# Statistics ahead of norm weights, two more banks for transposes, and the first feed-forward products around the last tiles' transposes, in an encoder layer on one core

## The chip, the cores and the metric

The kernel runs on one core of a Trainium2 chip. The metric is the device time of one execution in microseconds. TensorE is written PE, VectorE DVE, ScalarE ACT, GpSimd POOL, and SP is the engine that issues the DMAs.

## What is computed

One layer over 2048 tokens of width 1024, all in float32:

```python
def reference(x, mem, ...):
    x = layer_norm(x, ln0_g, ln0_b)
    for l in range(DEPTH):          # DEPTH = 1
        y = mixer(x, mem, w_in[l], ..., w_out[l])      # x @ w_in (1024 -> 1408), conv, pooling, attention, @ w_out
        x = layer_norm(DEEPNORM_ALPHA * x + y, ln1_g[l], ln1_b[l])
        y = conv_ffn(x, w_up[l], ...)                  # w_up 1024 -> 5632, conv of width 3, gated, w_down -> 1024
        x = layer_norm(DEEPNORM_ALPHA * x + y, ln2_g[l], ln2_b[l])
    return x
```

## The kernel before

Every float32 matrix product is made of three products of rounded parts: each operand is split into a high part (ACT copies it to fp32r, the names end in `hi`) and a low part (DVE subtracts the high part from the raw value, the names end in `lo`). So each stationary or moving operand needs one ACT copy and then one DVE subtraction before PE can use it. The order of the work on each engine is written out by hand; the engines wait for each other by semaphores, and each engine and SP's queue take their work strictly in this order.

**The opening and the input projection** (`project_phase`). The 2048 tokens are four chunks of 512, each of four tiles of 128 tokens (`TT`). For a tile, DVE's `layer_norm` takes the statistics (two `bn_stats`, one `bn_aggr`) and then subtracts the mean and multiplies with the norm weight (L389); POOL makes the reciprocal deviation; `layer_norm_end` (L395) multiplies with it and adds the norm bias. PE's `turn` transposes half a tile into one of the two PSUM banks `tp` (L264), ACT's `split_hi` copies the half out (L319), DVE's `split_lo` makes the low part (L401) and thereby frees the bank: `turn(c, i)` waits for the low part of half tile i-2. The weights `w_in` come in ten pieces (`load_w`), split by `weights_hi` (L324) and `weights_lo` (L406). In chunk 0 the first four of the eleven column tiles are projected in two halves of 256 tokens (`project_half`, L293), each half going through four weight pieces; the rest by `project` (L279). `turns_behind` says behind which column tile of a chunk the transposes of the next chunk stand: in chunk 0, behind the last four.

**The handover to the feed-forward part.** In the middle phase chunks are 256 tokens (`NCH` = 8, so the last is number 7, with two tiles). For its tile u, `residual` adds (L1616), `statistics` follows, POOL makes the deviation (`rstds`), ACT applies it (`norm`, L1341), DVE multiplies and adds the norm weights (`affine`, L1626 and L1627), PE transposes (`turn_x1`, L1073, into two banks), ACT copies out (`turned_x1`, L1459), four sums of the transposed quarters follow (`operand_sums`), and SP stores seven operands per chunk (`store_operands`).

The feed-forward products use a scheme of seven block products for what would be eight. A block (`Blk`) has seven stationary operands (`up.hi`, L2262, and `up.lo`, L2401; four of them from sums of raw quadrants, `held_sums`) and shares seven moving operands (`load_moving`, through three staging slots `mov_raw`; `up.moving_hi`, L2269, and `up.moving_lo`, L2405). Product j needs stationary and moving operand j. Product 0 goes to one bank, which ACT also copies to a second (`preset`); product 2 adds to this second one. `keep_u2` and `keep_u4` copy out intermediate results behind products 2 and 4, and product 6 waits for DVE's `up_c22` (L2428); ahead of that, `clear_edge` (L2604) writes to memory that the stores of the last operands must have left. PE's own order at the handover is at L1262 to L1277: the last projections, `turn_x1` of tile 0 of the last chunk, two matmuls that open banks, product 0, product 1, `turn_x1` of tile 1, then `rest` (products 2, 3, 4, product 0 of the second block, 5, 6). The four sums of the last chunk are made by POOL (`last_operand_sums`), those of all others by DVE.

## Time and profile before

| | us |
|---|---|
| median of 3 runs | 1945.98 |
| lowest and highest run | 1945.35, 1946.87 |
| profiled execution, its own time | 1944.67 |
| its span (first to last instruction) | 1943.0 |
| PE busy in the span | 1871.2 (96%) |
| DVE, ACT, POOL busy | 1474.6, 940.0, 221.2 |

The span is what the rows count from; the profiled execution's time is 1.67 us more, and the median of the runs is 1.31 us above that execution. PE is the busiest engine in nearly every part of the span, so time is to be looked for where PE stands idle or runs at the lower of its clock's levels. A row of the timeline has the start in us, the duration in us, the engine, the line of the kernel, the operation, what it writes and reads, and, in brackets, the idle time of the engine before it and what ended that. Where many like instructions are merged into one row, the duration is that of the group.

### The profile page before, as it was taken

The numbers are of one execution on the slowest core, as the hardware profiler recorded it, in microseconds if no ns is written. First come the engines' busy times: TensorE is split into PE (matmuls) and PEld (weight loads), VectorE is DVE, ScalarE is ACT, GpSimd is POOL, SyncE is SP. The second block draws the span as 40 slices with busy tenths as digits, with TensorE's granted clock in tenths as the row PEclk, the third lists the DMA queues.
The fourth block names the chain that finished last, engine by engine and source line by source line (L and its number), as shares of the span: only waits on it lengthen the run. The fifth ranks groups of instructions, "written<-read, shape, count | busy, mean of one in ns | idle before, by whom it ended". The sixth has DMA issues, their size and how long they took to land.

```text
span 1943.0 us, 26237 instructions
## 1 busy us (share of the span) xinstructions
PE 1871.2 (96%) x8722; PEld 1558.2 (80%) x8722; DVE 1474.6 (76%) x1927; ACT 940.0 (48%) x1598; POOL 221.2 (11%) x311
## 2 busy tenths in 40 slices
PE   6999999899999899999999899999999998999998
PEld 5788889688888688888888788888887786887886
DVE  6544228878887988888888987777878768567999
ACT  2311115746564565656556656555566335225231
POOL 1111014200000212121220020000000000000112
PEclk9999999999999999999999999999999999999999
DMA  6432226555345634434345432121215668457443
GB/s 227 168 109 71 60 79 212 185 160 187 133 153 186 253 124 143 141 135 140 130 143 175 148 140 108 76 86 76 97 69 179 226 211 292 165 173 278 177 155 127
DMA packets 171931, 296.13 MB, mean 152 GB/s; under 512 B 11728, under 2 KB 106192, under 8 KB 171856
## 3 DMA queue, kind: packets, MB, share of 16 engines
q1 hardware_dynamic: 171856, 295.18, 43.6%
q8 instruction: 42, 0.69, 0.1%
q14 instruction: 33, 0.27, 0.0%
HBM read 189.23 MB, written 105.91 MB: 152 GB/s over the span
## 4 chain that ended last, share of the span: by engine, by line
PE 62%; DVE 13%; DMA 4%; issue 3%; ACT 2%; SPq 0%; POOL 0%; DVEq 0%; ACTq 0%; POOLq 0%
PE banks L2200 49%; PE banks L1109 7%; DVE mov_lo L2405 2%; DVE sta_lo L2401 2%; DMA y_scratch<-up_and_out 2%; PE banks L1137 1%; DMA mov_raw<-in_w_down 1%; DVE up_and_out L2452 1%; PE banks L1042 1%; PE banks L1091 1%; ACT mov_hi L2269 1%; DVE up_and_out L2439 1%; PE banks L1118 1%; DVE up_and_out L2436 1%; PE banks L1062 1%
## 5 line engine op out<-in xcount | busy, mean ns | idle before, releaser
L2200 PE MATMUL banks<-mov_hi,sta_hi 128*128 128x512 f32 x1848 | 724.1, 392 | 25.0 <-DVE mov_lo L2405 9.1
L2200 PE MATMUL banks<-mov_hi,sta_lo 128*128 128x512 f32 x1848 | 721.7, 391 | 0.0
L2200 PE MATMUL banks<-mov_lo,sta_hi 128*128 128x512 f32 x1848 | 721.1, 390 | 0.0
L2200 PEld LDWEIGHTS banks<-mov_hi,sta_hi 128*128 128x128 f32 x1848 | 348.4, 189 | 106.9 <-issue 16.7
L2200 PEld LDWEIGHTS banks<-mov_hi,sta_lo 128*128 128x128 f32 x1848 | 348.1, 188 | 73.0
L2200 PEld LDWEIGHTS banks<-mov_lo,sta_hi 128*128 128x128 f32 x1848 | 348.5, 189 | 71.8
L2262 ACT ACTIVATE sta_hi<-sta_raw 128x512 fp32r<-128x512 f32 (+1 forms) x340 | 198.5, 611 | 144.3 <-PE banks L2200 98.2
L2401 DVE TENSOR_TENSOR sta_lo<-sta_raw,sta_hi 128x512 fp32r<-128x512 f32 (+1 forms) x340 | 224.0, 675 | 40.6 <-ACT sta_hi L2262 38.6
L279 PE MATMUL banks<-x0t_hi,win_hi 128*128 128x512 f32 x320 | 126.5, 395 | 1.6 <-DVE x0t_lo L401 1.6
L2291 ACT ACTIVATE half_sums<-banks 128x512 f32<-128x512 f32 x68 | 40.7, 598 | 179.4 <-PE banks L2200 179.4
L279 PE MATMUL banks<-x0t_hi,win_lo 128*128 128x512 f32 x320 | 124.8, 390 | 0.0
L279 PE MATMUL banks<-x0t_lo,win_hi 128*128 128x512 f32 x320 | 124.6, 389 | 0.0
L2439 DVE SCALAR_TENSOR_TENSOR up_and_out<-up_and_out,ffn_conv_w 128x1024 f32<-128x1024 f32 x88 | 113.1, 1285 | 11.2 <-DVE up_and_out L2436 5.5
L2432 DVE TENSOR_TENSOR up_and_out<-banks,half_sums 128x512 f32<-128x512 f32 x44 | 30.4, 691 | 115.9 <-PE banks L2200 115.9
L2334 ACT ACTIVATE up_and_out<-up_and_out,ffn_conv_b,ffn_conv_w 128x1024 f32<-128x1024 f32 x88 | 109.6, 1245 | 17.1 <-ACT up_carry L2317 7.8
L2436 DVE SCALAR_TENSOR_TENSOR up_and_out<-up_and_out,ffn_conv_w 128x1024 f32<-128x1024 f32 x88 | 112.5, 1278 | 0.0
L2282 ACT ACTIVATE half_sums<-banks 128x512 f32<-128x512 f32 x68 | 40.7, 598 | 143.6 <-PE banks L2200 130.1
L1109 PE MATMUL banks<-wout_hi,mix_hi 128*128 128x512 f32 x240 | 96.1, 400 | 1.0 <-DVE mix_lo L1604 1.0
L1109 PE MATMUL banks<-wout_hi,mix_lo 128*128 128x512 f32 x240 | 93.7, 390 | 0.0
L1109 PE MATMUL banks<-wout_lo,mix_hi 128*128 128x512 f32 x240 | 93.4, 389 | 0.0
L2401 DVE TENSOR_TENSOR sta_lo<-sta_sums,sta_hi 128x512 fp32r<-128x512 f32 (+1 forms) x136 | 92.9, 683 | 0.0
L2405 DVE TENSOR_TENSOR mov_lo<-mov_raw,mov_hi 128x2048 fp32r<-128x2048 f32 (+1 forms) x35 | 77.1, 2209 | 17.8 <-ACT mov_hi L2269 17.8
(242 smaller groups left out, 2706.0 us busy)
## 6 DMA issues: line engine op xcount, KB each, us to landing
sta_raw<-in_w_up SPq DMA_DIRECT2D x88, 512.0 KB, 4.2
hidden_scratch<-up_and_out SPq DMA_DIRECT2D x44, 512.0 KB, 2.6
y_scratch<-up_and_out SPq DMA_DIRECT2D x16, 1024.0 KB, 7.3
sta_raw<-hidden_scratch SPq DMA_DIRECT2D x32, 512.0 KB, 4.4
up_and_out<-y_scratch SPq DMA_DIRECT2D x16, 1024.0 KB, 4.9
x_operands<-x_operands_out SPq DMA_DIRECT2D x56, 256.0 KB, 4.3
mov_raw<-x_operands SPq DMA_DIRECT2D x14, 1024.0 KB, 7.8
mov_raw<-in_w_down SPq DMA_DIRECT2D x44, 256.0 KB, 4.6
```

Of the source, the lines that this page charges most:

```text
L279: last = pe.matmul(wb[:, done % 6, :], w, x, start=(k == 0 and i == 0), stop=(k == KT - 1 and i == 2))
L1109: last = pe.matmul(ps_y[:, b, :], w, x, start=(k == 0 and i == 0), stop=(k == KT - 1 and i == 2))
L2200: last = pe.matmul(psum, w, x, start=(start and k == 0 and i == 0), stop=(stop and k == m - 1 and i == 2), skip_group_check=True)
L2262: act.activation(sa_hi[j][:, 0:PAIRS[b.st], :], held(b, j), ACT.Copy).then_inc(sta_hi[j], 1)
L2282: act.activation(u[:, 0, :], ps[:, 2 + b.r, :], ACT.Copy).then_inc(u2, 1)
L2291: act.activation(u[:, 1, :], ps[:, 2 + b.r, :], ACT.Copy).then_inc(u4, 1)
L2334: act.activation(cv[:, w, :], ub[:, w, 0:HT], ACT.Identity, scale=fw[:, w, bass.ds(b.i, 1), 0], bias=fb[:, w, bass.ds(b.i, 1)]).then_inc(t ...
L2401: dve.tensor_tensor(sa_lo[j][:, 0:m, :], held(b, j), sa_hi[j][:, 0:m, :].bitcast(F32), ALU.subtract).then_inc(sta_lo[j], 1)
L2405: dve.tensor_tensor(moving(mv_lo, st, j), staged(st, j), moving(mv_hi, st, j).bitcast(F32), ALU.subtract).then_inc(mov_lo_ok, 1)
L2432: dve.tensor_tensor(tokens(b, VALUE, 0), bank(4 + b.r), u[:, 0, :].rearrange("p (q t) -> p q t", t=P), ALU.add).then_inc(c21, 1)
L2436: dve.scalar_tensor_tensor(out=cv[:, w, :], in0=ub[:, w, P:P + HT], scalar=fw[:, w, bass.ds(b.i, 1), 1], in1=cv[:, w, :], op0=ALU.mult, op ...
L2439: dve.scalar_tensor_tensor(out=cv[:, w, :], in0=ub[:, w, EDGE:EDGE + HT], scalar=fw[:, w, bass.ds(b.i, 1), 2], in1=cv[:, w, :], op0=ALU.mu ...
```

## The change

Seven things are changed.

1. The norm weight and the norm bias get a semaphore each; DVE takes the statistics of tiles 0 and 1 first, then multiplies by the weight (which waits for the weight alone), and waits for the bias only in `layer_norm_end`.
2. In chunk 0, half tiles 2, 3, 6 and 7 are transposed into two more banks (of the six `wb` of the projection), so that `turn(0, i)` waits only from i = 4 on, and for half tile i-4.
3. ACT's copies and DVE's subtractions of the opening are put into another order: transposed half tiles go ahead of weight pieces, and the seventh weight piece goes behind the last half tiles. Half tiles 4 to 7 are transposed behind piece 1 and in the middle of piece 3 of the first half.
4. The transposes of chunk 1 stand behind column tiles 6 to 9 and not 7 to 10, and the low parts of its half tiles are made between the norms and not after all of them.
5. At the handover PE opens the banks and makes product 0 ahead of `turn_x1` of tile 0, makes product 1 after waiting for one residual less, and products 2 and 3 ahead of `turn_x1` of tile 1.
6. ACT and DVE follow: `preset` ahead of the copies of tile 0, stationary and moving operand 3 ahead of `norm` and `affine` of tile 1, and `turned_x1` of tile 1 behind `keep_u2`.
7. The last operand sums go from POOL to DVE, and the load of moving operand 6 goes ahead of the stores of the last tile.

```diff
                 dst = mix_d[row:row + P, :].rearrange("p (r h q) -> p r h q", r=PHASES, h=2)[:, 4 * (c % 2):4 * (c % 2) + 4, c // 2, :]
                 sp.dma_start(dst, qb[:, t, :].rearrange("p (u q) -> p u q", u=TT)).then_inc(q_stored, 16)
 
+        def turned(c, i):
+
+            return wb[:, 4 + i % 2, :] if c == 0 and i % 4 >= 2 else tp[:, i % 2, :]
+
         def turns_behind(c, n):
 
             if c + 1 == NCH:
                 return ()
             if c == 0:
-                return (2 * (n - JT + TT), 2 * (n - JT + TT) + 1) if n >= JT - TT else ()
+                u = n - (JT - TT - 1)
+                return (2 * u, 2 * u + 1) if 0 <= u < TT else ()
             return (n - 1,) if 1 <= n <= 2 * TT else ()
 
         @block.sync
...
             load_x(0)
             load_x(1)
-            for n, v in enumerate((a["ln0_g"], a["ln0_b"])):
-                sp.dma_start(g_b[:, n, :], v.rearrange("(o n) -> o n", o=1).to_broadcast((P, D))).then_inc(gb_loaded, 16)
+            sp.dma_start(g_b[:, 0, :], a["ln0_g"].rearrange("(o n) -> o n", o=1).to_broadcast((P, D))).then_inc(g_loaded, 16)
+            sp.dma_start(g_b[:, 1, :], a["ln0_b"].rearrange("(o n) -> o n", o=1).to_broadcast((P, D))).then_inc(b_loaded, 16)
             for i in range(4):
                 load_w(i)
             load_x(2)
...
                 u, b = i // 2, i % 2
                 n = c * TT + u
                 pe.wait_ge(x0_ready, n + 1)
-                if 2 * TT * c + i >= 2:
+                if c == 0:
+                    if i >= 4:
+                        pe.wait_ge(lo_done, i - 3)
+                else:
                     pe.wait_ge(lo_done, 2 * TT * c + i - 1)
                 for k in range(4):
-                    last = pe.transpose(tp[:, b, k * P:(k + 1) * P], x0[:, n % RING, (4 * b + k) * P:(4 * b + k + 1) * P], ident[:, :])
+                    last = pe.transpose(turned(c, i)[:, k * P:(k + 1) * P], x0[:, n % RING, (4 * b + k) * P:(4 * b + k + 1) * P], ident[:, :])
                 last.then_inc(tp_ready, 1)
...
                                 last = pe.matmul(wb[:, n, tok], w, x, start=(k == 0 and i == 0), stop=(k == KT - 1 and i == 2), skip_group_check=True)
                         if half and piece == 3:
                             last.then_inc(proj, 1)
-                    if half == 0 and piece in (1, 2):
-                        turn(0, 2 * piece + 2)
-                        turn(0, 2 * piece + 3)
+                        if half == 0 and (piece, n) in ((1, 3), (3, 1)):
+                            turn(0, 3 + piece)
...
                 ins.then_inc(evac, 1)
 
             weights_hi(0)
-            weights_hi(1)
             split_hi(0, 0)
             split_hi(0, 1)
-            weights_hi(2)
             split_hi(0, 2)
             split_hi(0, 3)
-            for i in range(3, 7):
+            weights_hi(1)
+            for i in range(2, 6):
                 weights_hi(i)
             for i in range(TT, 2 * TT):
                 split_hi(0, i)
+            weights_hi(6)
             for c in range(NCH):
                 for n in range(JT):
...
                 dve.bn_stats(s[:, 6:12], x[:, 512:1024]).then_inc(ln_part, 1)
                 dve.wait_ge(ln_part, n + 1)
                 dve.bn_aggr(s[:, 12:14], s[:, 0:12]).then_inc(ln_var, 1)
+
+            def layer_scale(n):
+                s, x = st[:, n % RING, :], x0[:, n % RING, :]
                 dve.wait_ge(ln_var, n + 1)
-                dve.wait_ge(gb_loaded, 32)
+                dve.wait_ge(g_loaded, 16)
                 dve.scalar_tensor_tensor(out=x, in0=x, scalar=s[:, 12:13], in1=g_b[:, 0, :], op0=ALU.subtract, op1=ALU.mult).then_inc(ln_scaled, 1)
+
+            def layer_norm(n):
+                layer_stats(n)
+                layer_scale(n)
 
             def layer_norm_end(n):
                 s, x = st[:, n % RING, :], x0[:, n % RING, :]
+                dve.wait_ge(b_loaded, 16)
                 dve.wait_ge(ln_scaled, n + 1)
                 dve.wait_ge(ln_rstd, n + 1)
                 dve.scalar_tensor_tensor(out=x, in0=x, scalar=s[:, 14:15], in1=g_b[:, 1, :], op0=ALU.mult, op1=ALU.add).then_inc(x0_ready, 1)
...
                     layer_norm(c * TT + u)
                     layer_norm_end(c * TT + u)
 
-            layer_norm(0)
-            layer_norm(1)
+            layer_stats(0)
+            layer_stats(1)
+            layer_scale(0)
             layer_norm_end(0)
+            layer_scale(1)
             layer_norm_end(1)
+            lows(0, 0, 1)
             weights_lo(0)
-            lows(0, 0, 1)
+            lows(0, 2, 3)
             weights_lo(1)
-            lows(0, 2, 3)
             layer_norm(2)
-            layer_norm(3)
             layer_norm_end(2)
             weights_lo(2)
+            layer_norm(3)
             weights_lo(3)
             layer_norm_end(3)
             lows(0, 4, 5)
-            weights_lo(4)
             lows(0, 6, 7)
-            for i in range(5, 7):
+            for i in range(4, 7):
                 weights_lo(i)
             for c in range(NCH):
                 if c == 0:
                         weights_lo(i)
                     norms(1, 0)
                     norms(1, 1)
+                    lows(1, 0, 1)
                     gate(0, 1)
                     norms(1, 2)
+                    lows(1, 2, 3)
                     gate(0, 2)
                     norms(1, 3)
-                    lows(1, *range(2 * TT))
+                    lows(1, 4, 5, 6, 7)
                     continue
                 if c + 1 == NCH:
...
             sp.wait_ge(y_used, 2 * TT * NCH)
             up.load_raw(Blk(0, 1, 1))
             up.load_moving(0, 5)
+            up.load_moving(0, 6)
             store_x1(sp, NCH - 1, 1)
             sp.wait_ge(x1t_out, 4 * NCH)
             store_last_operands(sp, ((0, xt[:, 0, 0:4, :]), (3, xt[:, 0, 4:8, :]), (5, xt[:, 1, 4:8, :])), last_xt)
-            up.load_moving(0, 6)
             sp.wait_ge(x1_sums, 4 * NCH)
             store_last_operands(sp, ((1, xs[:, 0, :, :]), (4, xs[:, 1, :, :]), (2, xs[:, 2, :, :]), (6, xs[:, 3, :, :])), xop_stored)
             for s in x1_stored:
...
             pool.memset(half[:, 1:2], EPS).then_inc(half_ok, 1)
             pool.wait_ge(half_ok, 2)
-            def last_operand_sums():
-
-                pool.wait_ge(x1t_out, 4 * NCH)
-                operand_sums(pool, NCH - 1)
-
             def rstds(c):
...
                 project(NCH - 1, 1, n)
                 if n == 0:
                     turn_x1(NCH - 2, 1)
-            for b in range(2):
-                pe.wait_ge(x1t_out, (NCH - 2) * 4 + b + 3)
-            turn_x1(NCH - 1, 0)
             up = ffn.tensor(pe)
             first, second = Blk(0, 0, 0), Blk(0, 1, 1)
             up.open_banks()
             up.product_0(first)
-            pe.wait_ge(y_used, 2 * TT * NCH)
+            for b in range(2):
+                pe.wait_ge(x1t_out, (NCH - 2) * 4 + b + 3)
+            turn_x1(NCH - 1, 0)
+            pe.wait_ge(y_used, 2 * TT * NCH - 1)
             up.product_1(first)
+            up.products_2_3(first)
             turn_x1(NCH - 1, 1)
             up.rest(first, second)
...
             up.hi(first, 2)
             act.wait_ge(y_ready, 2 * TT * NCH)
             up.moving_hi(0, 2)
+            up.preset(first)
             turned_x1(NCH - 1, 0)
-            norm(NCH - 1, 1)
-            up.preset(first)
             up.hi(first, 3)
             up.moving_hi(0, 3)
-            turned_x1(NCH - 1, 1)
+            norm(NCH - 1, 1)
             up.hi(first, 4)
             up.moving_hi(0, 4)
             up.keep_u2(first)
+            turned_x1(NCH - 1, 1)
             up.hi(second, 0)
             up.hi(first, 5)
...
             residual(NCH - 1, 3)
             statistics(NCH - 1, 1)
             up.moving_lo(0, 2)
+            up.lo(first, 3)
+            up.moving_lo(0, 3)
             affine(NCH - 1, 1)
-            for j in (3, 4):
-                up.lo(first, j)
-                up.moving_lo(0, j)
+            up.lo(first, 4)
+            up.moving_lo(0, 4)
             up.lo(second, 0)
             up.lo(first, 5)
             up.moving_lo(0, 5)
             up.lo(first, 6)
+            dve.wait_ge(x1t_out, 4 * NCH)
+            operand_sums(dve, NCH - 1)
             dve.wait_ge(x1t_psum, 4 * NCH)
             for s in x1_stored:
                 dve.wait_ge(s, 16 * NCH)
...
             product(b, 1, ps[:, 4 + b.r, :], True, True)
 
+        def products_2_3(b):
+            pe.wait_ge(y_pre, 1)
+            product(b, 2, ps[:, 2 + b.r, :], False, True)
+            product(b, 3, ps[:, b.r, :], False, True)
+
         def rest(b, after):
-            x, y, z = ps[:, b.r, :], ps[:, 2 + b.r, :], ps[:, 4 + b.r, :]
-            pe.wait_ge(y_pre, 1)
-            product(b, 2, y, False, True)
-            product(b, 3, x, False, True)
```

## Rows read from the trace of the kernel before

**Rows 1.** The chain of work that ended last, share of the span by engine

```profile
PE 62%; DVE 13%; DMA 4%; issue 3%; ACT 2%; SPq 0%; POOL 0%; DVEq 0%; ACTq 0%; POOLq 0%
```

**Rows 2.** Timeline of PE in the opening

```profile
14.68 1.94 PE L264 MATMUL banks<-ident,x 128*128 128x128 f32 x8 [14.68 <-DVE x L395]
...
20.97 0.58 PE L293 MATMUL banks<-x0t_hi,win_hi 128*128 128x256 f32 x1 [1.41 <-DVE x0t_lo L401]
...
35.16 1.22 PE L264 MATMUL banks<-ident,x 128*128 128x128 f32 x8 [2.04 <-DVE x0t_lo L401]
```

**Rows 3.** Timeline of DVE in the opening

```profile
9.28 1.28 DVE L389 SCALAR_TENSOR_TENSOR x<-x,ln_stats,ln_gb 128x1024 f32<-128x1024 f32 x1 [2.88 <-DMA ln_gb<-in_ln_b]
...
13.27 2.47 DVE L395 SCALAR_TENSOR_TENSOR x<-x,ln_stats,ln_gb 128x1024 f32<-128x1024 f32 x2
...
16.79 1.27 DVE L401 TENSOR_TENSOR x0t_lo<-banks,x0t_hi 128x512 fp32r<-128x512 f32 x2
```

**Rows 4.** Timeline of ACT in the opening

```profile
10.55 1.06 ACT L324 ACTIVATE win_hi<-val_gate 128x1024 fp32r<-128x1024 f32 x1 [8.47 <-DMA val_gate<-in_w_in]
...
15.81 0.60 ACT L319 ACTIVATE x0t_hi<-banks 128x512 fp32r<-128x512 f32 x1 [2.84 <-PE banks L264]
...
33.17 0.63 ACT L324 ACTIVATE win_hi<-q_out 128x512 fp32r<-128x512 f32 x1 [8.86 <-DMA q_out<-in_w_in]
```

**Rows 5.** Timeline of SP, then DMA issues with KB and us to landing

```profile
1.72 0.42 SPq L199 DMA_DIRECT2D ln_gb<-in_ln_g  x1
...
ln_gb<-in_ln_g SPq DMA_DIRECT2D x1, 512.0 KB, 6.1
...
x<-in_x SPq DMA_DIRECT2D x2, 512.0 KB, 11.2
```

**Rows 6.** Stretches of L293: length, PE, PEld, granted clock, DMA share, GB/s

```profile
20.97:26.40 5.43, 5.43 (x25) 5.43 (x26) 1.00 0.02 7
...
35.16:40.20 5.04, 4.06 (x21) 4.09 (x22) 0.66 0.76 267
40.20:52.10 11.90, 11.90 (x101) 11.86 (x99) 1.00 0.30 95
```

**Rows 7.** Timeline of PE at the end of chunk 0

```profile
81.56 1.23 PE L264 MATMUL banks<-ident,x 128*128 128x128 f32 x8 [1.18 <-DVE x0t_lo L401]
...
97.11 0.50 PE L279 MATMUL banks<-x0t_hi,win_hi 128*128 128x512 f32 x1 [1.62 <-DVE x0t_lo L401]
```

**Rows 8.** Timeline of PE at the handover

```profile
635.57 1.94 PE L1073 MATMUL banks<-ident,x_out 128*128 128x128 f32 x8 [3.65 <-DVE x_out L1627]
...
653.14 0.47 PE L2200 MATMUL banks<-mov_hi,sta_hi 128*128 128x512 f32 x1 [1.32 <-DVE mov_lo L2405]
```

**Rows 9.** Groups of DVE instructions from 629 to 647: busy us, mean ns

```profile
L2405 DVE TENSOR_TENSOR mov_lo<-mov_raw,mov_hi 128x2048 fp32r<-128x2048 f32 x3 | 6.8, 2268 | 0.0
...
L2401 DVE TENSOR_TENSOR sta_lo<-sta_raw,sta_hi 128x512 fp32r<-128x512 f32 x3 | 2.1, 684 | 0.0
```

**Rows 10.** Groups of DVE instructions from 647.8 to 656.5

```profile
L2401 DVE TENSOR_TENSOR sta_lo<-sta_sums,sta_hi 128x512 fp32r<-128x512 f32 x2 | 3.6, 1785 | 0.0
```

**Rows 11.** Timeline of ACT and of DVE at the handover

```profile
638.10 2.24 DVE L2405 TENSOR_TENSOR mov_lo<-mov_raw,mov_hi 128x2048 fp32r<-128x2048 f32 x1
...
641.42 1.24 ACT L1341 ACTIVATE x_out<-x_out,ln_stats 128x1024 f32<-128x1024 f32 x1 [3.27 <-POOL ln_stats L59]
...
643.60 1.90 ACT L2269 ACTIVATE mov_hi<-mov_raw 128x2048 fp32r<-128x2048 f32 x1
...
661.98 0.63 DVE L2428 TENSOR_TENSOR up_and_out<-banks,half_sums 128x512 f32<-128x512 f32 x1
```

**Rows 12.** SP's issue of moving operand 3; landing of operands 3 and 5

```profile
633.52 0.65 SPq L2040 DMA_DIRECT2D mov_raw<-x_operands  x1
...
mov_raw<-x_operands SPq DMA_DIRECT2D x1, 1024.0 KB, 7.1
...
mov_raw<-x_operands SPq DMA_DIRECT2D x1, 1024.0 KB, 9.7
```

16 lines of the change are left out of this document (9 added, 7 removed).

## The prediction

> **What bounds the kernel now.** I read the shares of the chain of waits first: PE carries 62% of it and DVE 13% [rows 1]. The table gives PE 96% of the span, so a change of order gains only where PE stands idle or at its lower level, and only if nothing later absorbs the shift. Then I read the timelines of the three places that the diff touches.
>
> Opening: PE first works at 14.68, stands idle again ahead of the first projection at 20.97 and for 2.04 us ahead of 35.16 [rows 2]. DVE idles 2.88 us to 9.28 for the norm bias, though its next instruction reads only the weight [rows 3]. The 2.04 us wait starts on ACT: it stood 8.86 us, to 33.17, for the seventh weight piece, which is queued ahead of the transposed half tiles [rows 4]. Behind the wait the granted clock is 0.66 on average over 35.16 to 40.20; in the first stretch 25 matmuls of 256 columns took 5.43 us (0.217 each, the 1.2 GHz level), later 101 took 11.90 (0.118, the 2.4 GHz level) [rows 6]. Chunk 0's end: waits of 1.18 and 1.62 us for DVE's low parts [rows 7]. Handover: PE idle 3.65 us for tile 0 of the last chunk, eight transposes then take 1.94 us (1.22 at the full level in rows 2), and a 1.32 us wait for a moving operand at 653.14 [rows 2, 8]; but product 6 waits for DVE's `up_c22`, done at 662.6 [rows 11]. There DVE, not PE, sets the end.
>
> **Opening, step by step.** Statistics of tile 0 are over at 9.28 - 2.88 = 6.4. Those of tile 1 and its scaling lie between the end of the first scaling, 10.56, and 13.27: 2.7, of which scaling is 1.25, so statistics are 1.5 and now end at 7.9. The weight landed at 1.72 + 6.1 = 7.8 [rows 5]; scaling runs 8.0 to 9.2; the bias has landed by 9.28 [rows 3]; each end step is 1.23 (2.47 for two). Tile 0 is ready at 10.5, not about 14.5, tile 1 at 10.5 + 1.25 + 1.25 = 13.0. POOL's deviation of tile 1 has over 3 us. Transposes of tile 0 start near 10.7, those of tile 1 near 13.15, as no bank is waited for; each pair takes 1.94. ACT's piece 0 (10.55 to 11.6 [rows 4]) is still ahead, but the first half tile's copy starts 1.13 behind its transposes (14.68 to 15.81), at 11.8, so it costs nothing. The last copy ends near 15.7. DVE: end 13.0, two low parts 1.3, weight piece 1.1 (15.74 to 16.79 [rows 3]), low part 3 behind its copy at 16.0, low part 4 to 16.6. The first projection starts at 16.8 instead of 20.97: **-4.2**.
>
> Behind it PE takes 24 matmuls a piece: 5.1 at the lower level to 21.9, piece 1 2.85, half tiles 4 and 5 1.0, piece 2 2.85, half of piece 3 1.4, half tiles 6 and 7 1.0, the rest 1.4: 32.4. DVE, from 16.6: weight piece 1 1.2; tile 2 (landed 5.05 + 11.2 = 16.3 [rows 5]) 2.7 and its end, with POOL between, to 22.3; weight piece 23.5; tile 3 26.2; weight piece 27.35; end 28.6; low parts 4 and 5 29.9. PE needs tile 2 at 24.8, tile 3 at 30.0, piece 3 at 28.6: each is there, with 1.2 us to spare at the narrowest. Low parts 6 and 7 wait for their copies, to 32.6: a new wait of 0.2 to 0.3. So the 2.04 wait goes (**-2.0**), and the lower level behind it too: 16 matmuls x (0.217 - 0.118) = **-1.5**, against **+0.3**. Opening -7.4. Bounds: -5.5, if half a microsecond is lost at each of the four places where a row is extrapolated; -9, if the clock rises 1.6 us sooner than 5.4 us after the start.
>
> **Chunk 0's end.** Transposes of tile 0 of chunk 1 now stand one column tile (5.45 us) earlier; in the old trace tile 4 was ready 2.7 us ahead of that point. DVE carries the four tiles' norms in 4.6 us each, with two low parts (1.3) between, against PE's 5.45 + 0.9 for a column tile and its transposes; it is ahead at each. The last low parts are done some 3 us before PE needs them. Both waits go, and the 0.3 us by which the eight transposes at 81.56 were stretched: **-3.0** (bounds -2.4 and -3.3).
>
> **Handover.** PE no longer idles: banks and product 0 run from 631.8 to 635.0, tile 0's transposes at 635.6, product 1 to 639.2. But its idle time is not what counts; I follow ACT and DVE. DVE is unchanged to 640.3 [rows 11]. ACT now has moving operand 3 ahead of `norm`: its transfer lands at 633.5 + 7.1 = 640.6 [rows 12], the copy takes 1.9 [rows 11], so `norm` starts at 642.6, not 641.42: **a new wait**, behind which stand `affine`, the transposes of tile 1 and the last sums. DVE: low parts of operand 3 to 644.85, `affine` 2.45 (two instructions of 1024 columns, as in rows 3) to 647.3, operand 4 0.6 + 2.2 to 650.1, where product 4 starts, 3 us earlier than 653.14; second block's operand 0 and operand 5's low part to 651.3, moving operand 5 (its load issued when operand 2's low part ends, 640.3 [rows 11], landed 9.7 later [rows 12], copied by 652.3) to 654.5, operand 6's part 655.1 [durations: rows 9, less 0.08 for the overlap of neighbours]. The four sums, now here, are like low parts, 0.65 each: 2.6, to 657.7. Then moving operand 6 to 659.9, clear and add 1.05: 661.0 against 662.6. **-1.6.** That the sums cost DVE 2.6 us and it still ends earlier is because beside POOL's sums its subtractions took 1.79 instead of 0.68 us [rows 9, 10]: four of them, 4.4 us, come back. The stores behind the sums end near 662, and the first reader of their memory stood at 668. Bounds: +1.0 if the transfer lands 2.5 us later; -3.2 if it costs no wait.
>
> The Trainium skill's page "GPSIMD Engine Reference" says in its table of facts that POOL shares its SBUF interfaces with VectorE, with contention where DVE reads two SBUF inputs; rows 10 agree, and by it -1.6 would stand.
>
> **Sum.** -7.4 - 3.0 - 1.6 = -12.0. Projection, middle phase and feed-forward loops wait relative to PE, with no fixed hour, so I keep all of it. The span would be 1931.0, the profiled execution 1932.7; the median of runs lies 1.3 above, so 1945.98 - 12.0 = 1934.0.
>
> **Rivals.** (a) The handover gives nothing or loses up to 1 us: moving operand 3 or 5 lands late and holds `norm` or DVE. For: both landings stand in the sum as waits, and of two loads of 1 MB one took 7.1 and one 9.7 us [rows 12]; 2.5 us more for operand 3 is the bound above. Against: the order of issues is unchanged up to it. Time 1935.6 to 1936.6.
>
> (b) The new short waits at the handover (639.2 to 640.4, 643.2 to 644.9, 648.5 to 650.2) lower the clock. The 2.04 wait did, the 1.32 and 1.62 ones did not [rows 2, 7, 8]; mine go up to 1.7. Price: product 4 at the lower level takes 2.5 us more, of which DVE's queue hides 1.2: +1.3, to 1935.3; with the same thing once in the opening (+1.8) 1937.
>
> (c) The opening gains less: PE starts at 16.8, but the chip stays at the lower level through more of the 192 matmuls. By rows 6 each one costs 0.099 us. Ten more, +1.0. The gain is used up at 121 more; if all 168 behind the first piece and both pairs of transposes (+2.0) run so, it is 16.6 + 2.0 - 12.0 = +6.6: **slower, 1952.6**. Against: it rose after 5.4 us of work in the old trace. The skill's page "TensorE: Matmul & The Clock Gate", Part 1, says that the point of the rise differs from run to run with where the start falls; that would move the time by the bounds of the opening, not to this end.
>
> (d) The opening does not do what it says: ACT or DVE still waits for a weight piece that stands ahead (pieces 2 and 5 land while PE works). If the start stays 1.5 us short and the 2.04 wait stays half, -12.0 + 1.5 + 1.0 + 1.5 = -8.0: 1938.0.
>
> **How the numbers follow.** Forecast, all three parts within their bounds (1931 to 1936): 0.62; (a) 0.15; (b) 0.08; (d) 0.08; more gain than 15 us 0.03; (c) slower 0.02, nearly nothing left 0.02. Range 1930 to 1938.5, about 8 in 10 by these and the doubt in extrapolated rows. A measurement of this kernel tells changes over 0.2% (3.9 us) from none: faster 0.95, same 0.03, slower 0.02.
>
> **What would show it.** First transposes near 10.7, first projection near 16.8, no wait of PE over 0.5 us to the end of the first half, chunk 1 starting near 97.1 - 10.4 = 86.7, and no idle row there. At the handover, all times 10.4 earlier: transposes straight behind product 0, `norm` of tile 1 starting behind the copy of operand 3, three waits of 1 to 2 us between products, DVE's subtractions at 0.68 throughout, `up_c22` 12.0 earlier than before. Wrong would be: a granted clock of 0.5 beyond 25 us, ACT idle for a weight piece ahead of a half tile, or a later start of the feed-forward loops than 12 us early.

## The result, and the profile after

The changed kernel takes 1933.46 us (median of 4 runs, 1931.24 to 1933.50) against 1945.66 us beside it (4 runs, 1943.81 to 1946.87): 0.993 of the time, 95% interval 0.9918 to 0.9943. The forecast was 1934.0. The profiled execution took 1933.47 us, its span 1931.8 (before: 1944.67 and 1943.0). The chain of work that ended last hardly changes its shares [rows 1]:

```profile
PE 63%; DVE 12%; DMA 4%; issue 3%; ACT 3%; SPq 0%; POOL 0%; DVEq 0%; ACTq 0%; POOLq 0%
```

**Opening.** The timeline of PE, of DVE and of ACT in the changed kernel:

```profile
10.64 1.94 PE L273 MATMUL banks<-ident,x 128*128 128x128 f32 x8 [10.64 <-DVE x L412]
13.12 1.97 PE L273 MATMUL banks<-ident,x 128*128 128x128 f32 x8 [0.54 <-DVE x L412]
16.66 0.58 PE L302 MATMUL banks<-x0t_hi,win_hi 128*128 128x256 f32 x1 [1.56 <-DVE x0t_lo L418]
...
43.70 0.40 PE L288 MATMUL banks<-x0t_hi,win_hi 128*128 128x512 f32 x1
```

```profile
7.84 1.29 DVE L401 SCALAR_TENSOR_TENSOR x<-x,ln_stats,ln_gb 128x1024 f32<-128x1024 f32 x1
9.21 1.28 DVE L412 SCALAR_TENSOR_TENSOR x<-x,ln_stats,ln_gb 128x1024 f32<-128x1024 f32 x1
```

```profile
31.08 0.63 ACT L333 ACTIVATE win_hi<-q_out 128x512 fp32r<-128x512 f32 x1
```

The waits of [rows 2 to 4] are what to look for. The statistics now lie in front of the weight's landing, scaling starts at 7.84, and the first projection starts 4.31 us earlier than in [rows 2]. ACT copies the seventh weight piece without a wait where it stood for 8.86 us [rows 4], and the 2.04 us wait of [rows 2] is gone. In the stretches of L302 (length, PE, PEld, granted clock, DMA share, GB/s) PE is at work nearly throughout:

```profile
16.66:22.00 5.34, 5.34 (x29) 5.34 (x30) 1.00 0.84 310
22.00:34.00 12.00, 10.60 (x85) 10.03 (x84) 1.00 0.45 168
34.00:44.30 10.30, 9.86 (x83) 9.65 (x81) 1.00 0.59 189
```

From 16.66 to 20.8 some 18 matmuls are 0.213 us apart, the 1.2 GHz level; from there they are 0.12 apart, the 2.4 GHz level, and they stay so. The granted clock of the first stretch reads 1.00 all the same, as it does in [rows 6], so in the opening I go by the distance between starts. The first full column tile starts at 43.70; in the kernel before it did at 52.11.

**Chunk 0's end.** The four double transposes of chunk 1, two of which are shown, have no idle time before them. The second fence is the whole list of PE's waits up to 110 us (total us, times, longest); both lines are of the opening, and nothing answers to the 1.18 and 1.62 us of [rows 7]:

```profile
60.05 1.03 PE L273 MATMUL banks<-ident,x 128*128 128x128 f32 x8
...
79.09 1.04 PE L273 MATMUL banks<-ident,x 128*128 128x128 f32 x8
```

```profile
PE banks L273 <- DVE x L412: 11.2, 2, 10.6
PE banks L302 <- DVE x0t_lo L418: 1.6, 1, 1.6
```

**Handover.** PE, then ACT, then DVE; 624.86 is the last residual addition of the out-projection, 649.50 is `up_c22`'s addition (661.98 in [rows 11]):

```profile
629.41 0.47 PE L2218 MATMUL banks<-mov_hi,sta_hi 128*128 128x512 f32 x1 [1.09 <-DVE mov_lo L2425]
633.84 0.47 PE L2218 MATMUL banks<-mov_hi,sta_hi 128*128 128x512 f32 x1 [1.43 <-DVE mov_lo L2425]
639.04 0.47 PE L2218 MATMUL banks<-mov_hi,sta_hi 128*128 128x512 f32 x1 [1.31 <-DVE mov_lo L2425]
650.19 0.50 PE L2218 MATMUL banks<-mov_hi,sta_hi 128*128 128x512 f32 x1 [2.75 <-DVE up_and_out L2448]
```

```profile
629.45 1.92 ACT L2289 ACTIVATE mov_hi<-mov_raw 128x2048 fp32r<-128x2048 f32 x1 [2.48 <-DMA mov_raw<-x_operands]
631.27 1.23 ACT L1356 ACTIVATE x_out<-x_out,ln_stats 128x1024 f32<-128x1024 f32 x1
```

```profile
624.86 0.68 DVE L1631 SCALAR_TENSOR_TENSOR x_out<-x_in,banks 128x512 f32<-128x512 f32 x1
...
641.29 2.29 DVE L2425 TENSOR_TENSOR mov_lo<-mov_raw,mov_hi 128x2048 fp32r<-128x2048 f32 x1 [1.04 <-ACT mov_hi L2289]
...
646.76 2.28 DVE L2425 TENSOR_TENSOR mov_lo<-mov_raw,mov_hi 128x2048 fp32r<-128x2048 f32 x1
...
649.50 0.63 DVE L2448 TENSOR_TENSOR up_and_out<-banks,half_sums 128x512 f32<-128x512 f32 x1
```

PE's 3.65 us wait ahead of tile 0's transposes [rows 8] is gone; short waits of 1.1 to 1.4 us between products stand in its place. `norm` of tile 1 (631.27) starts behind the copy of operand 3, which itself stood for its transfer. DVE's subtractions take 0.68 us throughout, where [rows 10] have 1.785.

**Where the time came from.** Differences of starts in the two traces, changed kernel minus kernel before: first projection matmul -4.31; first full column tile -8.41; chunk 1's first evacuation -11.81; first residual addition of the out-projection -10.65; last one -11.08; `up_c22` -12.48; end of the span -11.20. So opening -8.4, chunk 0's end -3.4, handover -1.4, and 0.4 more between the first and the last residual addition, which I did not trace to a row; 1.2 us are given back in the middle phase and 1.3, net, between `up_c22` and the end.

### The profile page after: what moved, and what is told of

Its sections match the earlier page's. It is cut to its first block, busy times and chain, and to the rows that moved or that the text cites. A ratio compares the mean times of both kernels' runs of the same rounds, so it can differ in the third digit from the quotient of the medians.

```text
span 1931.8 us, 26236 instructions
## 1 busy us (share of the span) xinstructions
PE 1867.1 (97%) x8722; PEld 1554.8 (80%) x8722; DVE 1473.4 (76%) x1931; ACT 940.4 (49%) x1598; POOL 216.8 (11%) x307
## 4 chain that ended last, share of the span: by engine, by line
PE 63%; DVE 12%; DMA 4%; issue 3%; ACT 3%; SPq 0%; POOL 0%; DVEq 0%; ACTq 0%; POOLq 0%
PE banks L2218 49%; PE banks L1123 7%; DVE mov_lo L2425 2%; DVE sta_lo L2421 2%; DMA y_scratch<-up_and_out 2%; DMA mov_raw<-in_w_down 1%; PE banks L1151 1%; PE banks L1105 1%; PE banks L1056 1%; DVE up_and_out L2472 1%; ACT mov_hi L2289 1%; DMA mov_raw<-x_operands 1%; PE banks L1132 1%; DVE up_and_out L2459 1%; DVE up_and_out L2456 1%
```

## The experiments

The table puts the same marks of every profile side by side, as shifts in us from the profile of the kernel before. "c22 - residual" is the shift of `up_c22` less that of the last residual addition: the handover alone. Each shift is one start minus another, read from two timelines, and all of them are taken from one and the same profile of the kernel before, so what was particular to that execution is in every row. The rows of the changed kernel and of its repetition, and the two rows of the sums ahead of operand 5, show how far two executions of one kernel differ.

| version | full tile | chunk 1 | first residual | c22 - residual | end | median (runs) |
|---|---|---|---|---|---|---|
| changed kernel | -8.41 | -11.81 | -10.65 | -1.40 | -11.20 | 1933.46 (4) |
| changed, once more | -8.41 | -11.81 | -10.85 | -1.34 | -14.33 | 1931.27 (5) |
| opening only | -8.88 | -8.72 | -8.58 | -0.03 | -9.14 | 1935.89 (4) |
| chunk 0's end only | -0.33 | -3.73 | -2.26 | -0.04 | -2.93 | 1942.00 (10) |
| handover only | -0.31 | -0.45 | +1.09 | -1.29 | +0.84 | 1945.38 (10) |
| operand 3 loaded early | -8.30 | -11.69 | -10.91 | +0.70 | -8.84 | 1932.92 (4) |
| last sums on POOL | -8.61 | -12.01 | -11.01 | -1.10 | -14.13 | 1930.57 (1) |
| norm first | -7.80 | -11.20 | -11.27 | +3.38 | -6.53 | 1938.16 (1) |
| sums ahead of operand 5 | -7.27 | -10.67 | -10.49 | -2.33 | -14.40 | 1930.89 (4) |
| the same once more | -8.59 | -11.99 | -10.96 | -2.73 | -11.89 | 1932.79 (5) |
| weight waits for bias | -7.43 | -10.83 | -10.87 | -1.59 | -9.39 | 1935.31 (1) |
| two banks less | -7.61 | -11.03 | -10.19 | -1.47 | -11.16 | 1933.51 (1) |
| seventh piece ahead | -5.04 | -8.44 | -7.61 | -1.49 | -10.40 | 1934.26 (1) |

The kernel before beside them: 1944.71 (the first four experiments), 1947.04 (the next four), 1943.91 (the last four).

**One part alone: the opening, chunk 0's end, the handover.** Three kernels, each the kernel before with one part of the change. The opening has points 1 to 3 of the change; chunk 0's end has point 4, shown here; the handover has points 5 to 7.

```diff
-                return (2 * (n - JT + TT), 2 * (n - JT + TT) + 1) if n >= JT - TT else ()
+                u = n - (JT - TT - 1)
+                return (2 * u, 2 * u + 1) if 0 <= u < TT else ()
...
+                    lows(1, 0, 1)
...
+                    lows(1, 2, 3)
...
-                    lows(1, *range(2 * TT))
+                    lows(1, 4, 5, 6, 7)
```

> The kernel before with the opening part alone (own semaphores for weight and bias, statistics first, two more banks, the new order of pieces and half tiles in the first half); the transposes of chunk 1 and the handover stay as before. Theory: the opening's shift is made by its own waits, so the first column tile behind the two halves starts 8.4 us early as with the whole change, the two waits of 1.2 and 1.6 us at the end of chunk 0 stay, and the shift at the end of the input projection is 8.4 us; time about 1937.5 (8 us under the kernel before, 0.4%). Rival (the later waits take part of the shift back, as the whole change lost 1.2 us near 400 us of the span and another 1.3 in the down stages): the shift at the start of the feed-forward loops is under 7.5 us and the time over 1938.5.

Measured: ratio 0.9956 (0.9939 to 0.9972), 8.8 us less; the first full column tile comes 8.88 us earlier.

> The kernel before with the transposes of chunk 1 behind column tiles 6 to 9 and their low parts between the norms, nothing else. Theory: both waits of PE (1.18 and 1.62 us) go by themselves, without the earlier opening: chunk 1 starts 3.4 us earlier than in the kernel before, and the time is about 1942.5. Rival (the gain needs the earlier norms of the opening): a wait of PE for a normalised tile or a low part of over 0.5 us shows up at the transposes, and the shift is under 2 us.

Measured: ratio 0.9982 (0.9972 to 0.9991), 2.7 us less. Between the full tile and chunk 1, -3.73 + 0.33 = -3.40, the same as in the changed kernel; 1.5 us of it are gone by the first residual addition.

> The kernel before with the handover part alone. Theory: DVE, held by the landing of moving operand 3 (its copy on ACT starts at about 640.2 us of the span and its low part at about 642), sets the end, and product 6 starts 1.8 us earlier than before: time about 1944, a change that may not be told from none. Rival (PE's removed idle time of 3.65 us and its clock are what counts): product 6 starts over 3.5 us earlier.

Measured: ratio 1.0002 (0.9992 to 1.0011), no change. Its own part is there (-1.29), but the same profile lost 1.5 us in the middle phase, ahead of the edit, and 1.7 between `up_c22` and the end. I had expected 1.8 us for this part. The spans' shifts add up: -9.14 - 2.93 + 0.84 = -11.2, and the span of the whole change is 11.2 shorter; but the repetition of the changed kernel was 14.3 shorter, so that this fits to a tenth is luck. The medians add to -8.8 - 2.7 + 0.7 = -10.8, against 12.2 measured in another series. The marks are the better test: chunk 0's end gives 3.40 alone and 3.40 with the rest, the handover 1.29 alone and 1.34 to 1.59 with the rest.

**Moving operand 3 loaded early.** The wait of 2.48 us on ACT is for operand 3's transfer. The load goes ahead of the stores that stand in front of it in SP's queue:

```diff
-            store_operands(sp, NCH - 2)
             up.load_moving(0, 3)
+            store_operands(sp, NCH - 2)
```

> The changed kernel with one line of SP's queue moved: the load of moving operand 3 ahead of the seven stores of the chunk before the last, where it waits only for the low part of moving operand 0. Theory: in the changed kernel ACT waits 2.48 us and DVE 1.54 us for this transfer and all behind it (norm of tile 1, its affine, operand 4) is late by it; issued near 611 us, where the DMA engines idle, it lands before 620, ACT's copy of operand 3 starts at about 627, the only wait left for norm is POOL's, and product 6 starts 1.3 to 2.5 us earlier than in the changed kernel: time about 1931.8. Rival (DVE's own work, not the transfer, sets the end; or the seven stores and the next operands land later by what the load takes): product 6 starts less than 0.5 us earlier.

The wait for the transfer went, and `up_c22` still came 2.1 us later relative to the residual (+0.70 against -1.40). ACT, POOL, PE and the stretch 638.60 to 643.00 (length, busy PE, PEld, DVE, ACT, POOL, granted clock, DMA) of this version:

```profile
626.31 1.92 ACT L2289 ACTIVATE mov_hi<-mov_raw 128x2048 fp32r<-128x2048 f32 x1
631.90 1.24 ACT L1356 ACTIVATE x_out<-x_out,ln_stats 128x1024 f32<-128x1024 f32 x1 [3.67 <-POOL ln_stats L59]
```

```profile
626.85 2.12 POOL L54 TENSOR_TENSOR ln_stats<-ln_stats,rstd_consts 128x1 f32<-128x1 f32 x1 [9.24 <-DVE ln_stats L1637]
629.05 0.88 POOL L56 TENSOR_TENSOR ln_stats<-ln_stats,rstd_consts 128x1 f32<-128x1 f32 x1
630.03 1.83 POOL L59 TENSOR_SCALAR ln_stats<-ln_stats 128x1 f32<-128x1 f32 x1
```

```profile
629.07 0.47 PE L2218 MATMUL banks<-mov_hi,sta_hi 128*128 128x512 f32 x1 [1.08 <-DVE mov_lo L2425]
635.71 1.09 PE L1087 MATMUL banks<-ident,x_out 128*128 128x128 f32 x8 [0.85 <-DVE x_out L1642]
638.61 0.77 PE L2218 MATMUL banks<-mov_hi,sta_hi 128*128 128x512 f32 x1 [1.80 <-DVE mov_lo L2425]
```

```profile
638.60:643.00 4.40, 4.39 (x10) 3.46 (x11) 3.36 (x3) 1.73 (x1) 0.00 (x0) 0.50 0.59 230
```

DVE now subtracts operand 3 at 629.44, beside POOL's operations of one column; the last of them takes 1.83 us instead of 0.27 in the changed kernel, and `norm` waits for it. This uses up what the early load gave: product 4 starts 14.09 us behind the last residual addition (638.61 and 624.52), in the changed kernel 14.18 (639.04 and 624.86). The loss comes behind it. The waits of PE ahead of product 4 have grown to 0.85 and 1.80, and product 4 runs at the lower level (granted 0.50); ACT stands 3.78 us for it at 644.11 (0.78 in the changed kernel), and DVE 2.60 us for ACT at 645.25. My theory, that the transfer holds the handover, fell. The new wait named in the prediction is real, but with it gone POOL stands in the same place. The profiled execution was the slowest of the four (1935.84; the others 1931.65 to 1933.90), and only this one shows its clock, so whether the lower level follows from the edit or belongs to this execution is open. The median (1932.92) is not to be told from the changed kernel's.

**Norm first.** Undoes one reordering of point 6: `norm` and `affine` of tile 1 go back ahead of operand 3.

```diff
+            norm(NCH - 1, 1)
             up.hi(first, 3)
             up.moving_hi(0, 3)
-            norm(NCH - 1, 1)
...
+            affine(NCH - 1, 1)
             up.lo(first, 3)
             up.moving_lo(0, 3)
-            affine(NCH - 1, 1)
```

> The changed kernel with the last tile's second norm and affine put back ahead of moving operand 3's copy and subtraction. My theory: ScalarE stands some 1.5 to 3.3 us for GpSimd's statistic ahead of the norm, so the copy of operand 3 starts 1 to 2 us later than in the changed kernel (at 633.7), product 4's first matmuls with it, and c22 comes 0.5 to 1.5 us later. Rival (the order is worth nothing, since the transfer of operand 3 holds the copy in either order): c22 within 0.3 us of the changed kernel's, counted from the last residual addition of the out-projection.

```profile
636.24 0.61 PE L2218 MATMUL banks<-mov_hi,sta_hi 128*128 128x512 f32 x1 [4.67 <-DVE mov_lo L2425]
```

```profile
634.00:639.60 5.60, 3.36 (x8) 2.67 (x9) 4.90 (x3) 1.89 (x2) 0.00 (x0) 0.72 0.90 299
```

Theory and rival both had too little. PE, which in this order is already behind product 2, stands 4.67 us and then works at the lower level; `up_c22` comes 4.8 us later than in the changed kernel (3.38 + 1.40), and a further 1.85 us is lost by the middle of the feed-forward loops, of which 650 to 660 us with a granted clock of 0.67 is the first piece. The order of point 6 carries the handover.

**Last sums on POOL.** Undoes the first half of point 7.

```diff
+            def last_operand_sums():
+                pool.wait_ge(x1t_out, 4 * NCH)
+                operand_sums(pool, NCH - 1)
...
+            last_operand_sums()
...
-            dve.wait_ge(x1t_out, 4 * NCH)
-            operand_sums(dve, NCH - 1)
```

> The changed kernel with only its third part's move of the four operand sums of the last chunk undone: GpSimd forms them again, as in the kernel before. My theory: what the sums on VectorE cost in the changed kernel (4 x 0.69 = 2.8 us, of which little waits) is less than what the same sums on GpSimd do to VectorE beside them (subtractions 1.79 instead of 0.69 us and 3.4 instead of 2.29 us for some of those between 636 and 648 us). So c22's addition, counted from the last residual addition of the out-projection, comes 1 to 2.5 us later than in the changed kernel, and the four subtractions beside the sums show their longer times. Rival: GpSimd's work is hidden beside VectorE's and c22 comes up to 2.8 us earlier; the move was then a cost and not a gain.

```profile
638.20 1.64 DVE L2425 TENSOR_TENSOR sta_lo<-sta_raw,sta_hi 128x512 fp32r<-128x512 f32 x1
639.76 1.78 DVE L2425 TENSOR_TENSOR sta_lo<-sta_sums,sta_hi 128x512 fp32r<-128x512 f32 x1
641.46 3.38 DVE L2429 TENSOR_TENSOR mov_lo<-mov_raw,mov_hi 128x2048 fp32r<-128x2048 f32 x1
644.76 1.76 DVE L2425 TENSOR_TENSOR sta_lo<-sta_raw,sta_hi 128x512 fp32r<-128x512 f32 x1
```

The slowing is as expected (1.64 to 1.78 instead of 0.69, 3.38 instead of 2.29), but `up_c22` moved by 0.3 us only, which is no more than the unaltered handover differs between profiles (-1.29 to -1.59). The sum: the four subtractions cost 0.95 + 1.09 + 1.09 + 1.07 = 4.2 us more; the four sums no longer cost DVE its 2.7; and DVE's 1.04 us wait for ACT's copy of operand 5 is filled. 4.2 - 2.7 - 1.04 = 0.5. My expectation had left this wait out.

**Sums ahead of operand 5.** The wait of 1.04 us at 641.29 can be filled with the sums themselves:

```diff
             up.lo(first, 5)
-            up.moving_lo(0, 5)
-            up.lo(first, 6)
             dve.wait_ge(x1t_out, 4 * NCH)
             operand_sums(dve, NCH - 1)
+            up.moving_lo(0, 5)
+            up.lo(first, 6)
```

> The changed kernel with VectorE's four sums of the last chunk's operands put ahead of the low parts of moving operand 5 and of the stationary operand 6. In the changed kernel VectorE stands 1.04 us for ScalarE's copy of operand 5 at 641.29 and forms the sums only after it. My theory: the first of the sums fill this wait; VectorE ends the same list of work up to 1.0 us earlier, or the subtraction of operand 5 comes 1.7 us later and TensorE waits for it; since the products up to 5 have less work left than this, c22 comes 0.3 to 1.0 us earlier, and the time is 1932.5 to 1933.5, not to be told from the changed kernel by the timed runs. Rival: product 5 waits for its low part longer than TensorE has work, the clock falls to its lower level as it did in the version with operand 3 loaded early (granted 0.50 from 638.6 to 643), and c22 comes 1 to 2 us later.

```profile
642.60 0.69 DVE L758 TENSOR_TENSOR x_operands_out<-x_operands_out 128x512 f32<-128x512 f32 x1
643.21 2.28 DVE L2425 TENSOR_TENSOR mov_lo<-mov_raw,mov_hi 128x2048 fp32r<-128x2048 f32 x1
...
648.76 0.62 DVE L2448 TENSOR_TENSOR up_and_out<-banks,half_sums 128x512 f32<-128x512 f32 x1
```

The wait is gone, `up_c22` comes 0.9 us earlier, and in the second profile 1.3. Its first series gave 1930.89 us (ratio 0.9924, 0.9908 to 0.9941), which looked like a gain over the changed kernel. So both ran in one series on the same chip:

> The changed kernel once more, unaltered, beside the version with the sums ahead on the same chip. Both theories: 1931 to 1934 us, as before. It also shows whether what the profiles give back at the stage boundaries behind 1590 us (1.3 us in the changed kernel's profile, nothing in the profile of the version with the sums ahead) belongs to the one execution or to the kernel.

> The version with the last chunk's sums ahead of moving operand 5, once more, beside the changed kernel on the same chip. My theory: c22 comes 0.9 us earlier, counted from the last residual addition (as in its first profile), and the median is 0.9 to 2.6 us below the changed kernel's. Rival: its first median (1930.89) came from fewer lower-clock stretches that either kernel can have, and the two medians lie within 0.9 us of each other.

Changed kernel 1931.27 us (1930.37 to 1932.93; ratio 0.9932, 0.9918 to 0.9945), sums ahead 1932.79 us (1930.47 to 1933.69; 0.9937, 0.9923 to 0.9950). The rival holds: the two are not to be told apart, though the version has the shorter handover in both profiles. Where the difference is covered can be seen at the start of the down projection. First the changed kernel, in its first profile, with the stretch 1625 to 1630:

```profile
1625.79 0.79 PE L2218 MATMUL banks<-mov_hi,sta_hi 128*128 128x512 f32 x1 [3.12 <-DVE up_and_out L2472]
...
1625.00:1630.00 5.00, 4.21 (x10) 3.34 (x11) 5.00 (x10) 1.60 (x4) 0.00 (x0) 0.50 0.56 222
```

then the same kernel in its second profile:

```profile
1626.34 0.50 PE L2218 MATMUL banks<-mov_hi,sta_hi 128*128 128x512 f32 x1 [3.11 <-DVE up_and_out L2472]
...
1625.00:1630.00 5.00, 3.66 (x16) 3.04 (x17) 5.00 (x9) 2.69 (x6) 0.00 (x0) 1.00 0.67 257
```

The same wait, 3.12 and 3.11 us, before the same matmul (the work ahead of it differs a little, with a gap of 0.60 us in the one and 0.34 in the other, 6 us earlier): behind the one the clock is at the lower level, behind the other at the full one. The shifts at a mark ahead of that place and at one behind it (ACT's copies into `half_sums` at 1622.99 and 1706.94 in the kernel before) are -13.88 to -12.72 in the one and -13.11 to -14.98 in the other, 3.0 us apart, and the ends are 3.1 apart. So the 1.3 us given back behind `up_c22` belong to one execution, not to the change. Two more steps there stand in all thirteen profiles, 0.3 to 1.5 us gained from 1589 to 1606 and 0.3 to 3.2 lost from 1783 to 1833 (times of the kernel before); this points to the one profile that all of them are measured from.

**The opening, three edits undone one at a time.** DVE's scaling waits for the bias too:

```diff
                 dve.wait_ge(g_loaded, 16)
+                dve.wait_ge(b_loaded, 16)
```

> The changed kernel with one wait added: VectorE's weight scaling of the first tiles waits for ln_b as well as for ln_w, as the norm weights did before. It takes away what the split of the two waits gives and leaves the order (statistics ahead) and the banks. My theory: in the changed kernel the first scaling starts at 7.84 and the first bias addition at 9.21; with ln_b landing at 9.2 to 9.3 the first scaling moves to about 9.3, so the first turn on TensorE starts 1.3 to 1.5 us later (10.64 to about 12.0) and the half projection 1.0 to 1.5 us later (16.66 to about 17.9), with the projection's first full matmul (43.70) as much later. Rival: the half projection's start is set by transfers and ScalarE's list (pool_in at 19, w_in) rather than by the first tile's norm, and moves by less than 0.5 us.

```profile
9.12 1.28 DVE L402 SCALAR_TENSOR_TENSOR x<-x,ln_stats,ln_gb 128x1024 f32<-128x1024 f32 x1 [1.39 <-DMA ln_gb<-in_ln_b]
```

The scaling moves 1.3 us, and the first projection with it (17.93, +1.27), the full tile +0.98. But the full tile is no sure mark for one edit: in the eight profiles whose opening is that of the changed kernel it lies between -7.27 and -8.88, since the matmuls come to 0.12 us apart at times from 16.8 to 23.1. The shift of the scaling and of the first projection is the edit's; at the full tile it can't be told from none. The two further banks taken away:

```diff
-            return wb[:, 4 + i % 2, :] if c == 0 and i % 4 >= 2 else tp[:, i % 2, :]
+            return tp[:, i % 2, :]
...
-                if c == 0:
-                    if i >= 4:
-                        pe.wait_ge(lo_done, i - 3)
-                else:
+                if 2 * TT * c + i >= 2:
```

> The changed kernel with its two further banks for chunk 0's transposes taken away and the old waits put back: the transposes share two banks again, in chunk 0 too. My theory: the first half of the second tile's transposes must wait for the low parts of the first tile, which VectorE forms only after both tiles' norms (at 12.99 to 14.2), so the second tile's transposes start some 0.5 to 1.5 us later than at 13.12 and the half projection 0.5 to 1.5 us later than at 16.66; at chunk 0's end the wait of 1.2 us that the kernel before had there comes back for the most part. Rival: VectorE's statistics of the tiles set the second tile's transposes in any case, and the banks gave nothing at the opening (less than 0.3 us).

```profile
13.86 1.94 PE L270 MATMUL banks<-ident,x 128*128 128x128 f32 x8 [1.24 <-DVE x0t_lo L415]
```

The banks are worth 0.7 us to the second tile's transposes and 0.6 to the first projection (0.2 to 0.7 against the other profiles of this opening); the 0.8 at the full tile is again within what profiles of one opening differ by. The rest of my expectation fell: at chunk 0's end only 0.2 us of waits came back, and that part is -11.03 + 7.61 = -3.42 as ever. It is point 4, the place of the transposes and of their low parts, that removed those waits, not the banks. The seventh piece ahead:

```diff
-            for i in range(2, 6):
+            for i in range(2, 7):
                 weights_hi(i)
...
-            weights_hi(6)
```

> The changed kernel with one line's place undone: ScalarE's high part of the seventh piece of the input weights goes back ahead of the copies of tiles 2 and 3. My theory: that piece's load waits for low parts that VectorE forms late, so ScalarE stands, the copies of the turned tiles 2 and 3 come late, TensorE waits about 2 us in the half projection as before (2.04 us at 35.16) and then works again at its lower clock for some microseconds; the first full product (43.70 in the changed kernel) comes 2 to 3.5 us later. Rival: the earlier statistics have already made room, the piece is there in time, and the place of this line is worth less than 0.5 us.

```profile
30.51 0.63 ACT L333 ACTIVATE win_hi<-q_out 128x512 fp32r<-128x512 f32 x1 [7.03 <-DMA q_out<-in_w_in]
...
34.20 0.58 PE L302 MATMUL banks<-x0t_hi,win_hi 128*128 128x256 f32 x1 [2.66 <-DVE x0t_lo L417]
```

The wait of [rows 4] is back (7.03 us on ACT), PE stands 2.66 us, 12 matmuls behind it run 0.213 apart, and the full tile comes 3.37 us later than in the changed kernel. Of the three, this alone is outside the spread at the full tile: the place of one line costs some 3 us (2.2 by the nearest profile of this opening, 3.8 by the farthest).

What of this reaches the out-projection? For the three, +0.98, +0.80 and +3.37 at the full tile have become -0.22, +0.46 and +3.04 at the first residual addition, and the version with the sums ahead, 1.14 behind there, is 0.16 behind here. Where the microsecond goes is seen at the first out-projection matmul behind PE's longest wait there, in the kernel before, the changed kernel, the version with the sums ahead and its second profile:

```profile
388.74 0.77 PE L1118 MATMUL banks<-wout_hi,mix_hi 128*128 128x512 f32 x1 [4.25 <-ACT x_operands_out L1360]
376.76 0.77 PE L1132 MATMUL banks<-wout_hi,mix_hi 128*128 128x512 f32 x1 [5.57 <-ACT x_operands_out L1375]
378.05 0.76 PE L1132 MATMUL banks<-wout_hi,mix_hi 128*128 128x512 f32 x1 [4.25 <-ACT x_operands_out L1375]
376.55 0.76 PE L1132 MATMUL banks<-wout_hi,mix_hi 128*128 128x512 f32 x1 [5.56 <-ACT x_operands_out L1375]
```

Up to here nothing is lost: the changed kernel starts it 11.98 us early, the version with the sums ahead 10.69, as much as at chunk 1 (-11.81, -10.67). The loss is behind it, where matmuls run 0.43 us apart, the 1.2 GHz level, before they come to 0.23: 5 such in the kernel before, 12 in the changed kernel, each 0.2 us longer. Seven more cost 1.4 us; with the 0.2 gained ahead of this place (-11.81 to -11.98) that is the 1.2 given back. The version with the sums ahead has 6 of them in its first profile and 11 in its second, and loses 0.2 and 1.0 us; the version with the handover alone, which at this place is still the kernel before, has 13 and loses 1.5. So this microsecond, too, differs between executions of one kernel; the opening's gain is not absorbed by a wait. What sets the number of slow matmuls is open.

## Why the prediction was right

**The opening, -7.4, measured -8.41.** The starts hold to a tenth: transposes 10.64 and 13.12 (10.7, 13.15), first projection 16.66 (16.8). The seventh piece and the 2.04 us wait went as said; the new wait for the last two low parts is there, 0.3 us long. The term that was too small is the clock: it rose after 4.1 us and 18 matmuls, not after 5.4 us and 25 [rows 6], which is 7 or 8 matmuls at 0.095 us, -0.7; the transposes of the kernel before at 35.16 were stretched by 0.2 as well, which I did not count. Both lie within the bound of -9. This term is not one number: the eight profiles of this opening give -7.27 to -8.88, with the rise at 16.8 to 23.1 us. That the part is the cause is shown by the version with it alone (-8.9), and the version with the seventh piece ahead shows what that piece's place removes: a wait of 2.66 us and 12 matmuls at the lower level. The wait for the bias and the banks are shown as far as the first projection (1.3 and 0.6 us). The rest of the reordering (statistics of tile 1 ahead, half tiles ahead of weight pieces) was not undone by itself.

**Chunk 0's end, -3.0, measured -3.40** in every version that has it. It is just outside my bound of -3.3, and the term that was too small is the price of a wait. I took the 1.18 and 1.62 us of idle time of [rows 7]. But matmuls that don't wait start 0.23 us apart and last 0.39, so each starts before the one ahead has ended, and idle time counts only from that end. By starts the two places cost 1.33 and 1.87 us more than in the changed kernel; with 0.19 for the stretched transposes that is the 3.4.

**The handover, -1.6, measured -1.3 to -1.6** in the six profiles that have it unaltered. Taken back by the 11.08 us of the last residual addition, the forecast times are: `norm` 631.5 (measured 631.27), product 4 639.0 (639.04), operand 5 copied 641.2 (DVE takes it up at 641.29), `up_c22` 649.9 (649.50). The price of the sums on POOL (four subtractions, 4.4 us) was measured as 4.2. But what this move is worth by itself is 0.3 us in one profile, within what the unaltered handover differs by, since POOL's slowing had filled a wait of DVE; the gain of this part hangs on the order of ACT and DVE around operand 3.

**Sum.** That all of the gain is kept behind each part held for the waits, but not for the clock: stretches at the lower level in the middle phase and behind `up_c22` gave back 1.2 and 1.3 us in this execution. The span came 11.2 us shorter, not 12.0; the opening and chunk 0's end, 1.4 us better than forecast, made up for most of it. I also put the median 1.3 us above the profiled execution, and it lay on it (1933.46 and 1933.47). That the forecast of 1934.0 came within 0.6 us is therefore partly luck: the same kernel in another series had 1931.27. What the runs bear out is the size of the three parts.

**The rivals.** (a) is refuted: the part gives what was forecast, though the handover alone does not show in a timed comparison. (b) did not occur at the three waits that it names, which in the changed kernel are 1.09, 1.43 and 1.31 us long (1.10, 1.52 and 1.33 in its second profile) and left the clock alone; it is seen one step away, in the version with operand 3 early and in that with the norm first. I had not named the wait ahead of product 6: behind 2.75 us the clock stayed in the first profile, behind 2.69 in the second it fell for part of 650 to 655 (granted 0.68), which cost 0.6 us. (c) is refuted in its size: the clock rose earlier than before in the changed kernel, and at its latest, in one profile of this opening, at 23.1 us, which left a gain of 7.3. (d) is refuted by the starts.

## What to carry to other kernels

When work is put ahead of a wait, look at what else stands behind the same wait on the neighbouring engines: one weight piece in the wrong place on ACT cost some 3 us, while the other two edits of the opening that were undone can't be told from none at the same mark. Taking one wait out of a chain that runs in step on three engines need not shorten it: without the 2.5 us for a transfer, POOL's operations met a DVE subtraction, and the next product started no earlier. And compare profiles at marks close around the edit, with no change of the clock between them: chunk 0's end came out as 3.39 to 3.42 us in every profile that has this part, the handover as 1.3 to 1.6, but the opening, with a rise of the clock inside, as 7.3 to 8.9. Profile the same kernel twice before a microsecond is given a cause; one lower-clock stretch elsewhere weighed up to 3 us.

## What the runs showed of the hardware

POOL's last operation on one column (128x1, L59) took 0.27 us by itself and 1.83 us beside a DVE subtraction of 2048 columns; the slowing goes both ways (DVE 0.69 to 1.78, 2.29 to 3.38 beside POOL's sums of 512 columns). It is less a slower pace than a wait for the end: the 1.83 us end at 631.86, the subtraction at 631.72, and the changed kernel's first one (L54, 2.12 us) at 629.31, the subtraction beside it at 629.26. The Trainium skill's page "GPSIMD Engine Reference" has in its table of facts that the two share SBUF interfaces, and the traces agree; that an operation of one column suffers as well I had not expected.

The same wait of 3.1 us before the same matmul left the clock at 2.4 GHz in one execution and at 1.2 GHz in another. In the opening of the version whose weight waits for the bias, the clock rose inside the second tile's transposes (1.66 us instead of 1.97), the first projection matmuls were 0.12 us apart, and then 0.21 until 22.4:

```profile
14.41 1.66 PE L273 MATMUL banks<-ident,x 128*128 128x128 f32 x8 [0.54 <-DVE x L413]
...
18.27 0.28 PE L302 MATMUL banks<-x0t_hi,win_lo 128*128 128x256 f32 x1
...
19.36 0.42 PE L302 MATMUL banks<-x0t_lo,win_hi 128*128 128x256 f32 x1
```

PE had been without work for 1.87 us ahead of the projection. The Trainium skill's page "TensorE: Matmul & The Clock Gate", Part 1, says that the point of the rise differs from run to run, and the two profiles of the version with the sums ahead agree: in one and the same kernel the matmuls came to 0.12 us apart at 23.1 us and at 20.3. The waits of 3.1 us above show the same of the fall.
